# More tile buffers, another queue, a row sum on VectorE and another item order in the opening quarters of a decoder trunk

## The chip, the cores and the metric

The kernel runs on one core of a Trainium2 chip. The metric is device time in microseconds (us) of one execution; lower is better. A profiled execution gives the trace: one record for each instruction of TensorE (PE, with its weight loads as PEld), VectorE (DVE), ScalarE (ACT), GpSimd (POOL) and the DMA issues of SyncE (SP) and ACT. SPq and ACTq are the sequencers that issue DMAs.

## The reference, cut to what matters

A decoder trunk of two layers for one sequence of 256 tokens of width 2048, all in float32: layer 0 mixes with gated linear attention, layer 1 with latent attention, each followed by a gated feed-forward with a width-3 convolution. Every norm is modulated by a shift and a scale that come from a conditioning vector c:

```python
c_act = jax.nn.silu(c)
mod = c_act @ mod_w[i] + mod_b[i]          # (2048) @ (2048, 12288)
sh_m, sc_m, g_m, sh_f, sc_f, g_f = jnp.split(mod, 6, axis=-1)
h = modulate(rmsnorm(x, norm_mix_g[i]), sh_m, sc_m)   # h * (1 + scale) + shift
proj = h @ w_in                            # first product of layer 0
```

Here only the beginning counts: the shift and the scale of layer 0's first norm (two 2048 x 2048 blocks of mod_w, 32 MB), x normalised and modulated, and the first product with gla_w_in (q, then k). The convolution's taps and biases (ffn_conv_w, ffn_conv_b) are small and used much later.

## The kernel before, in words

**Precision.** A float32 product is three matmuls of rounded halves: w_hi (made by ACT, `hi`, line 746) and w_lo (made by DVE, `lo`, line 1166) of each weight item, h_hi and h_lo of the activations. A weight item is 4 row tiles by 512 columns, 1 MB, in a ring of four slots (`raw`); a load into a slot waits until the item four before it has been used (`load_item`, line 527).

**The opening.** It is divided into four quarters q, each for 512 of the 2048 columns of shift and scale. A quarter has eight modulation tiles of 1 MB, `PRE_TILES`: for each of four row groups i, kind 0 (shift) and kind 1 (scale). Tile m sits in slot m % 5; two slots are in `mods`, three in `pre_s2`. `load_pre` (line 545) waits, for tile m, until tile m - 5 has been consumed. Twenty of the 32 tiles are summed by DVE (`gather_pre`, lines 1347 and 1349): four instructions that multiply a row tile by a column of c and add it to `acc`. The other twelve, kind 1 with i < 3, are summed by TensorE (`pre_scale`, line 1944): eight records of one weight column against 512 columns, giving a row in PSUM.

At a quarter's end DVE copies TensorE's row to SBUF (`row_s`, line 1390), in space that x occupied. TensorE then adds up the 128 partitions of `acc` (`pre_reduce`, line 1956), for kind 0 and for kind 1; for kind 1 each of the four matmuls on `acc` is followed by a one-row matmul that adds `row_s` (line 1959). DVE turns both into the columns of `ab` (`pre_columns`, lines 1361 and 1363). ACT makes h_hi (line 761), DVE h_lo (lines 1240, 1245), for four row tiles of the input. With these, items 2q and 2q + 1 of gla_w_in can be multiplied (`q_item`).

**Order by hand.** Each engine has its own written-out order. DVE in quarter q: tiles 8q, 8q+2, 8q+4, `lo` of item 2q, tile 8q+6, `lo` of item 2q+1, tile 8q+7, the row, the columns, h_lo. TensorE: `pre_scale` 0, the first item of the quarter before, `pre_scale` 1, transposes of the normalised input, `pre_scale` 2, both reductions, the second item of the quarter before. SP issues all loads in one order: tiles 0, 1, then small rows and x, 2, 3, item 0, 4, 5, item 1, 6, 7, 8 to 11, item 2, 12, 13, item 3, 14, 15, then eight loads of the convolution's rows (each 88 rows of 512 bytes, 44 KB), 16 to 19, item 4, 20, 21, item 5, 22, 23, 24 to 27, item 6, 28, 29, item 7, 30, 31. ACT: squares of x, the normalised second half, then items 0 and 1 of `hi`, and so on.

After the quarters TensorE multiplies items 5, 6, 7, then the gate's item 8, and from item 9 on each item's load is released by the item four before it. The order after that is not touched.

Of the kernel before, what the change touches and what calls it, by code (L numbers as in the profile page):

```python
# [29 lines left out]
P = 128  # L30
RAW = 4
AHEAD = 3
MODS = 2
PRE = 5
KT_ITEM = 4
W = 512
ITEM = KT_ITEM * W
# [97 lines left out]
def yoco_kernel(nc, x, c, positions, mod_w, mod_b, norm_mix_g, norm_ffn_g, gla_w_in, gla_w_gate2,  # L135
# [49 lines left out]
    crow = place("crow", S2 + 2048, [KT, 2, P], F32)  # L185
    cvrow = place("cvrow", S2 + 4096, [2 * FT, 8, P], F32)
    pre_s2 = place("pre_s2", S2 + 8192, [P, PRE - MODS, D], F32)
    row_s = place("row_s", X, [1, W], F32)

    qk_t = place("qk_t", X, [P, 2 * DKT, T], F32)  # L190
    v_sb = place("v_sb", S2, [P, TT, D], F32)
# [115 lines left out]
    with ExitStack() as ctx:  # L307
# [6 lines left out]

        raw_in = [sem(f"raw_in{i}") for i in range(RAW)]
        mod_in = [sem(f"mod_in{i}") for i in range(MODS)]
        pre_in = [sem(f"pre_in{i}") for i in range(PRE)]
        pre_dve = sem("pre_dve")
        pre_pe = sem("pre_pe")
        pre_on = sem("pre_on")  # L320
# [91 lines left out]
                 "down10": 20, "down11": 24, "down12": 28, "end": 32}  # L412
        def pre_slot(m):

            k = m % PRE
            v = mods[:, k, :] if k < MODS else pre_s2[:, k - MODS, :]
            return v.rearrange("p (j n) -> p j n", j=KT_ITEM)

        PRE_TILES = [(q, i, kind) for q in range(4) for i in range(4) for kind in (0, 1)]

        def on_pe(m):
            _, i, kind = PRE_TILES[m]
# [87 lines left out]
        def _(sp):  # L510
# [18 lines left out]
            def load_mod(n, g, kt):  # L529

                if n < MODS:
                    sp.wait_ge(pre_dve, 20)
                else:
                    sp.wait_ge(mod_used, n - MODS + 1)
                w, col = mod_source(g)
                sp.dma_start(mods[:, n % MODS, :], w[kt * P:kt * P + P, col:col + D])\
                    .then_inc(mod_in[n % MODS], 16)

            def load_pre(m):

                if m >= PRE:
                    sp.wait_ge(pre_pe if on_pe(m - PRE) else pre_dve, taken(m - PRE))
                q, i, kind = PRE_TILES[m]
                w, col = mod_source(kind)
                sp.dma_start(pre_slot(m), columns(w, i, col + q * W)).then_inc(pre_in[m % PRE], 16)

            def columns(w, q, col, k_tiles=KT_ITEM, width=W):

# [53 lines left out]
            for n, src in enumerate(where):  # L602
                if n < 8:
                    for m in range(4 * n if n else 2, 4 * n + 4) if n % 2 == 0 else (4 * n, 4 * n + 1):
                        load_pre(m)
                if n - AHEAD == a["mla"].item + 2:

                    sp.wait_ge(tp_done, a["norm4"].tp + 2)
                for m in mod_at.get(n - AHEAD, ()):
                    load_mod(*m)  # L610
                if n == a["r"].item + 8:


                    sp.wait_ge(ms_done, made(a["diag"].ms + 1))
                    sp.wait_ge(xq_made, 2 * len(UNITS))
                    sp.dma_start(x_sb[:, :, :], x.rearrange("o (t p) d -> p (o t) d", p=P)).then_inc(x_in, 16)
                if n == a["down12"].item:

                    sp.wait_ge(mod_used, 12 * KT)
                    sp.dma_start(mods[:, 0, :], final_norm_g.partition_broadcast(P)).then_inc(fin_in, 16)  # L620
                load_item(n, src)
                if n < 8 and n % 2:
                    for m in (4 * n + 2, 4 * n + 3):
                        load_pre(m)
                if n == 3:
                    for layer in range(2):
                        for k in range(3):
                            sp.dma_start(cvrow[:, 4 * layer + k, :],
                                         ffn_conv_w[layer, k].rearrange("(r p) -> r p", p=P)).then_inc(taps_in, 16)
                        sp.dma_start(cvrow[:, 4 * layer + 3, :],  # L630
                                     ffn_conv_b[layer].rearrange("(r p) -> r p", p=P)).then_inc(taps_in, 16)
                if n == 8:

                    sp.dma_start(wg2[0:RANK, :], gla_w_gate2[0]).then_inc(wg_in, 16)
                    sp.dma_start(wg2[RANK:RANK + 1, :], gla_b_gate).then_inc(wg_in, 16)
# [98 lines left out]
        def _(act):  # L734
# [124 lines left out]
            act.wait_ge(x_in, 16)  # L859
            squares("norm0", x_sb, xn)  # L860
            normalised("norm0")
            for q in range(4):
                hi(2 * q)
                hi(2 * q + 1)
                if q < 3:
                    act.wait_ge(pre_on, q + 1)
                else:
                    act.wait_ge(columns_on, 1)
                split(a["norm0"].tp + 2 * q, 2, (h_hi,), (ab[:, A_OF["mix0"]],), (ab[:, A_OF["mix0"] + 1],), 2 * q)
                if q == 1:  # L870

                    act.wait_ge(ang_made, 1)
                    act.activation(sin[:, :, :], ang[:, 0], ACT.Sin).then_inc(sin_made, 1)
                    act.activation(cos[:, :, :], ang[:, 1], ACT.Sin).then_inc(sin_made, 1)
# [281 lines left out]
        def _(dve):  # L1156
# [180 lines left out]
            def gather_pre(m):  # L1337

                q, i, kind = PRE_TILES[m]
                dve.wait_ge(pre_in[m % PRE], 16 * (m // PRE + 1))  # L1340
                if taken(m) > 1:
                    dve.wait_ge(pre_dve, taken(m) - 1)
                total, tile_ = acc[:, kind, q * W:(q + 1) * W], pre_slot(m)
                for j in range(KT_ITEM):
                    ck = c_col[:, KT_ITEM * i + j:KT_ITEM * i + j + 1]
                    if j == 0 and (i == 0 or kind == 1):
                        ins = dve.tensor_scalar(total, tile_[:, j, :], ck, None, ALU.mult)
                    else:
                        ins = dve.scalar_tensor_tensor(total, tile_[:, j, :], ck, total, ALU.mult, ALU.add)
                    step.link(ins) if j < KT_ITEM - 1 else ins.then_inc(pre_dve, 1)  # L1350
# [23 lines left out]
            for q in range(4):  # L1374
                for i in range(4):
                    gather_pre(8 * q + 2 * i)
                    if q == 0 and i == 1:
                        dve.wait_ge(tp_done, 2)
                        for t, rows in enumerate((104, P, 96)):
                            ins = dve.tensor_copy(pcol[:, t, 0:rows], tp[:, 1, t * P:t * P + rows])  # L1380
                            step.mark(ins) if t < 2 else ins.then_inc(tp_free, 1)
                        dve.wait_ge(tp_free, 2)
                        normalised("norm0", x_sb, xn)
                    if i >= 2:
                        lo(2 * q + i - 2)
                gather_pre(8 * q + 7)
                if q == 0:
                    dve.wait_ge(xn_made, XN_FROM["norm0"] + TT)
                dve.wait_ge(pre_pe, 3 * q + 3)
                dve.tensor_copy(row_s[:, :], ms[0:1, (a["pre"].ms + 3 * q) % 2, :]).then_inc(ms_free, 1)  # L1390
                pre_columns(q)
                split("norm0", 2, (h_lo,), (h_hi,), (ab[:, A_OF["mix0"]],), (ab[:, A_OF["mix0"] + 1],), 2 * q)
                if q == 0:
                    angles()
                if q == 2:
                    dve.wait_ge(sin_made, 2)
                    step.link(dve.tensor_tensor(cos[:, :, :], cos[:, :, :], cos[:, :, :], ALU.mult))
                    step.link(dve.tensor_scalar(cos[:, :, :], cos[:, :, :], -2.0, 1.0, ALU.mult, ALU.add))
# [385 lines left out]
        def _(pe):  # L1784
# [150 lines left out]
            def pre_scale(q, i):  # L1935

                m = 8 * q + 2 * i + 1
                pe.wait_ge(pre_in[m % PRE], 16 * (m // PRE + 1))
                if i == 0:
                    pe.wait_ge(tp_free, 1)  # L1940
                o, tile_ = ms_open(a["pre"].ms + 3 * q), pre_slot(m)
                for j in range(KT_ITEM):
                    kt = KT_ITEM * i + j
                    ins = pe.matmul(o[0:1, :], c_col[:, kt:kt + 1], tile_[:, j, :], start=kt == 0,
                                    stop=kt == 3 * KT_ITEM - 1)
                ins.then_inc(pre_pe, 1)

            def pre_reduce(q):

                fill = a["pre"].ms + 3 * q + 1  # L1950
                for kind in range(2):
                    pe.wait_ge(pre_dve, 5 * q + 4 + kind)
                    o = ms_open(fill + kind)
                    for b in range(4):
                        c0 = q * W + b * P
                        ins = pe.matmul(o[:, b:b + 1], acc[:, kind, c0:c0 + P], ones[:, 0:1],
                                        start=True, stop=kind == 0)
                        if kind:
                            ins = pe.matmul(o[:, b:b + 1], row_s[0:1, b * P:(b + 1) * P], ones[0:1, 0:1],
                                            start=False, stop=True)  # L1960
                    ins.then_inc(ms_done, 1)

            def pre_turn(q):
# [14 lines left out]
            for q in range(4):  # L1978
# [3 lines left out]
                pre_scale(q, 1)  # L1982
                pre_turn(q)
                pre_scale(q, 2)
                pre_reduce(q)
                if q:
                    q_item(q - 1, 1)
            for ch in range(2):
                q_item(3, ch)

# [341 lines left out]
```

## Time and profile before

| | |
|---|---|
| median of 3 runs | 2476.84 us (2469.88 to 2478.08) |
| profiled execution | 2479.71 us |
| its span, first to last instruction | 2478.0 us |
| mean granted TensorE clock | 0.965 |
| TensorE busy | 95% |
| DVE busy | 74% |
| DMA | 255 GB/s on average |

The profiled execution's own time stands 1.7 us above its span and 2.9 us above the median of the runs. Its page gives busy time by engine, and the trace behind it answers for any stretch of time. The stretch of the change is 0 to 152 us: the four quarters end (second reduction read by DVE) at 47.9, 81.7, 113.1 and 143.6 us.

### The profile page before, as it was taken

How to read it: one execution, taken by the hardware profiler on the slowest of the kernel's cores; microseconds unless marked ns; L12 is line 12 of the kernel's file. 1: busy time of each engine (PE TensorE's matmuls, PEld its weight loads, DVE VectorE, ACT ScalarE, POOL GpSimd, SP SyncE). 2: the span in 40 equal slices, each digit the busy share in tenths (PEclk: the TensorE clock that was granted, in tenths of full speed). 3: DMA queues.
4: the chain of work that ended last, by engine and by line, in shares of the span. 5: the costliest groups of instructions: out<-in, count | busy, mean ns of one | idle time of the engine just before them, and what ended most of it. 6: DMA issues, size and time to landing. Idle time of an engine off the chain costs nothing.

```text
span 2478.0 us, 27045 instructions
## 1 busy us (share of the span) xinstructions
PE 2358.1 (95%) x10904; PEld 1912.0 (77%) x10904; DVE 1838.5 (74%) x1731; ACT 1102.2 (44%) x1195; POOL 114.7 (5%) x145
## 2 busy tenths in 40 slices
PE   5898999899999999999999899999999999999998
PEld 2567878577887788888887688877887888878876
DVE  5766987677888887878897878787777546555565
ACT  2124443334545335543444555435565345444453
POOL 0010650000000000000000000000000000000000
PEclk8898999898999999999999899998999999999999
DMA  8955769576997997869986656685866555555554
GB/s 322 336 202 220 257 236 371 189 277 235 359 334 272 340 354 279 327 243 367 343 315 244 220 174 213 247 321 186 325 252 239 184 194 182 186 172 190 187 174 148
DMA packets 259808, 632.91 MB, mean 255 GB/s; under 512 B 23505, under 2 KB 32745, under 8 KB 233978
## 3 DMA queue, kind: packets, MB, share of 16 engines
q1 hardware_dynamic: 258842, 626.26, 70.3%
q10 hardware_dynamic: 864, 5.24, 0.5%
q8 instruction: 70, 1.15, 0.2%
q14 instruction: 32, 0.26, 0.0%
HBM read 629.36 MB, written 2.10 MB: 255 GB/s over the span
## 4 chain that ended last, share of the span: by engine, by line
PE 78%; DVE 8%; DMA 7%; ACT 3%; issue 3%; SPq 1%; POOL 1%; DVEq 0%; POOLq 0%; ACTq 0%
PE gm L1805 21%; PE gm L1806 21%; PE gm L1812 20%; PE tp L1846 2%; PE gm L1797 2%; DMA raw<-in_ffn_w_down_dram 2%; PE gm L1799 2%; PE gm L1798 2%; DVE w_lo L1166 2%; ACT w_hi L746 2%; DVE acc L1183 2%; DVE conv L1546 1%; DMA raw<-in_gla_w_o_dram 1%; DMA mods<-in_mod_w_dram 1%; DMA raw<-in_gla_w_in_dram 1%
## 5 line engine op out<-in xcount | busy, mean ns | idle before, releaser
L1166 DVE TENSOR_TENSOR w_lo<-raw,w_hi 128x2048 fp32r<-128x2048 f32 (+1 forms) x378 | 851.3, 2255 | 375.5 <-ACT w_hi L746 374.3
L746 ACT ACTIVATE w_hi<-raw 128x2048 fp32r<-128x2048 f32 (+1 forms) x378 | 703.6, 1863 | 740.2 <-DMA raw<-in_ffn_w_up_dram 241.0
L1805 PE MATMUL gm<-w_hi,h_hi 128*128 128x512 f32 x1816 | 726.9, 400 | 0.2 <-DVE h_lo L1245 0.2
L1806 PE MATMUL gm<-w_hi,h_lo 128*128 128x512 f32 x1816 | 715.7, 394 | 0.0
L1812 PE MATMUL gm<-w_lo,h_hi 128*128 128x512 f32 x1816 | 448.8, 389 | 0.0
L1183 DVE SCALAR_TENSOR_TENSOR acc<-mods,c_col,acc 128x2048 f32<-128x2048 f32 x180 | 422.3, 2346 | 5.2 <-DMA mods<-in_mod_w_dram 4.6
L1805 PEld LDWEIGHTS gm<-w_hi,h_hi 128*128 128x128 f32 x1816 | 346.6, 191 | 77.1 <-issue 5.0
L1806 PEld LDWEIGHTS gm<-w_hi,h_lo 128*128 128x128 f32 x1816 | 346.3, 191 | 71.3 <-issue 1.0
L1812 PEld LDWEIGHTS gm<-w_lo,h_hi 128*128 128x128 f32 x1816 | 340.8, 188 | 70.9
L1805 PE MATMUL gm<-w_hi,a_hi 128*128 128x512 f32 x692 | 279.3, 404 | 11.7 <-DVE a_lo L1569 9.6
L1806 PE MATMUL gm<-w_hi,a_lo 128*128 128x512 f32 x692 | 274.9, 397 | 0.0
L1546 DVE SCALAR_TENSOR_TENSOR conv<-tp,cv_col,conv 128x255 f32<-128x255 f32 (+1 forms) x352 | 152.4, 477 | 85.2 <-ACT conv L982 82.0
L1812 PE MATMUL gm<-w_lo,a_hi 128*128 128x512 f32 x692 | 172.5, 390 | 0.0
L1805 PEld LDWEIGHTS gm<-w_hi,a_hi 128*128 128x128 f32 x692 | 133.0, 192 | 45.0 <-DVE a_lo L1569 12.6
L1806 PEld LDWEIGHTS gm<-w_hi,a_lo 128*128 128x128 f32 x692 | 133.1, 192 | 29.0 <-issue 1.4
L1812 PEld LDWEIGHTS gm<-w_lo,a_hi 128*128 128x128 f32 x692 | 130.3, 188 | 27.2
L752 ACT ACTIVATE u<-gm 128x1024 f32<-128x1024 f32 x76 | 77.4, 1019 | 152.8 <-PE gm L1812 145.5
L982 ACT ACTIVATE conv<-tp,cv_col 128x256 f32<-128x256 f32 x176 | 88.2, 559 | 119.6 <-PE tp L1846 119.2
L684 POOL TENSOR_TENSOR sq<-sq 128x2 f32<-128x2 f32 x4 | 4.6, 1156 | 1872.4 <-ACT tp L778 1872.4
L715 POOL TENSOR_TENSOR ex<-ex,qk_t 128x512 f32<-128x512 f32 x32 | 79.6, 2508 | 124.7 <-ACT ex L912 124.7
L761 ACT ACTIVATE h_hi<-tp,ab 128x256 fp32r<-128x256 f32 x64 | 32.0, 562 | 93.4 <-DVE ab L1363 55.7
L1797 PE MATMUL gm<-w_hi,h_hi 128*128 128x512 f32 x136 | 60.2, 442 | 10.2 <-DVE w_lo L1166 5.7
(257 smaller groups left out, 2166.4 us busy)
## 6 DMA issues: line engine op xcount, KB each, us to landing
raw<-in_ffn_w_up_dram SPq DMA_DIRECT2D x176, 1024.0 KB, 4.9
mods<-in_mod_w_dram SPq DMA_DIRECT2D x174, 1024.0 KB, 7.2
raw<-in_ffn_w_down_dram SPq DMA_DIRECT2D x64, 1024.0 KB, 5.2
raw<-in_gla_w_in_dram SPq DMA_DIRECT2D x48, 1024.0 KB, 5.3
mods<-in_kv_mod_w_dram SPq DMA_DIRECT2D x32, 1024.0 KB, 6.9
raw<-in_ffn_w_down_dram SPq DMA_DIRECT2D x32, 768.0 KB, 4.3
pre_s<-in_mod_w_dram SPq DMA_DIRECT2D x18, 1024.0 KB, 11.1
raw<-in_gla_w_o_dram SPq DMA_DIRECT2D x16, 1024.0 KB, 9.0
```

What stands on the lines that cost most here:

```text
L715: pool.tensor_tensor(f, f, s, ALU.mult).then_inc(xq_made, 1)
L746: act.activation(w_hi[:, k % RAW, 0:words], raw[:, k % RAW, 0:words], ACT.Copy).then_inc(hi_made, 1)
L752: act.activation(dst, gm[:, par] if src is None else src, func).then_inc(u_made, 1)
L982: ins = act.activation(conv[:, j % 2, side, :], tp[:, bank, side * T:(side + 1) * T], ACT.Identity, scale=cv_col[:, layer, 2, cs], bias=cv ...
L1166: dve.tensor_tensor(w_lo[:, k % RAW, 0:words], raw[:, k % RAW, 0:words], w_hi[:, k % RAW, 0:words].bitcast(F32), ALU.subtract).then_inc(lo ...
L1183: return dve.scalar_tensor_tensor(total, tile_, ck, total, ALU.mult, ALU.add)
L1546: ins = dve.scalar_tensor_tensor(v, tp[:, bank, side * T:(side + 1) * T - shift], cv_col[:, layer, tap, cs], v, ALU.mult, ALU.add)
L1797: pe.matmul(o, hi_s[:, kt, tok], wh[:, j, :], start=kt == 0, stop=False)
L1798: pe.matmul(o, hi_s[:, kt, tok], wl[:, j, :], start=False, stop=False)
L1805: pe.matmul(o, hi_s[:, kt, tok], wh[:, j, :], start=kt == 0, stop=False)
L1806: pe.matmul(o, lo_s[:, kt, tok], wh[:, j, :], start=False, stop=False)
L1812: return pe.matmul(o, hi_s[:, kt, tok], wl[:, j, :], start=False, stop=kt == total - 1)
```

## The change

The ring of modulation tiles gets two more slots, `pre_x`, in the space of x, which is free once x has been normalised. Tiles 0 to 9 keep their slots; tile 10 and 11 go to the new ones (after a wait until x has been read) and from tile 12 on a tile takes the slot of the tile seven before it. The eight loads of the convolution's rows leave SP's order and are issued by ACT, after the normalised input and before item 0's `hi`. `row_s` goes: DVE adds TensorE's row, which is in PSUM, into partition 0 of `acc`, and the reduction of kind 1 has no one-row matmuls; DVE first waits for its own last sum. In TensorE's order the second item of the quarter before comes ahead of the reductions in quarters 1 and 2, and stays behind them in quarter 3. The loads of the first two later modulation tiles wait for TensorE's last `pre_scale` too.

```diff
+PRE_LATE = 2
-    row_s = place("row_s", X, [1, W], F32)
+    pre_x = place("pre_x", X, [P, PRE_LATE, D], F32)
 def pre_slot(m):
-            k = m % PRE
-            v = mods[:, k, :] if k < MODS else pre_s2[:, k - MODS, :]
+            k = PRE_SLOT[m]
+            v = mods[:, k, :] if k < MODS else pre_s2[:, k - MODS, :] if k < PRE else pre_x[:, k - PRE, :]
+        PRE_SLOT = [m % PRE if m < 2 * PRE else (m - 2 * PRE + PRE) % (PRE + PRE_LATE) for m in range(len(PRE_TILES))]
+        def pre_landed(m):
+            return 16 * PRE_SLOT[:m + 1].count(PRE_SLOT[m])
 def load_mod(n, g, kt):
                 if n < MODS:
                     sp.wait_ge(pre_dve, 20)
+                    sp.wait_ge(pre_pe, 12)
 def load_pre(m):
-                if m >= PRE:
-                    sp.wait_ge(pre_pe if on_pe(m - PRE) else pre_dve, taken(m - PRE))
+                before = [k for k in range(m) if PRE_SLOT[k] == PRE_SLOT[m]]
+                if before:
+                    sp.wait_ge(pre_pe if on_pe(before[-1]) else pre_dve, taken(before[-1]))
+                elif PRE_SLOT[m] >= PRE:
+                    sp.wait_ge(xn_made, XN_FROM["norm0"] + TT)
 SP's order of loads
-                if n == 3:
-                    for layer in range(2):
-                        for k in range(3):
-                            sp.dma_start(cvrow[...], ffn_conv_w[layer, k]...).then_inc(taps_in, 16)
-                        sp.dma_start(cvrow[...], ffn_conv_b[layer]...).then_inc(taps_in, 16)
 ACT
             normalised("norm0")
+            for layer in range(2):
+                for k in range(3):
+                    act.dma_start(cvrow[...], ffn_conv_w[layer, k]...).then_inc(taps_in, 16)
+                act.dma_start(cvrow[...], ffn_conv_b[layer]...).then_inc(taps_in, 16)
 DVE, at a quarter's end
-                if q == 0:
-                    dve.wait_ge(xn_made, XN_FROM["norm0"] + TT)
+                dve.wait_ge(pre_dve, 5 * q + 5)
                 dve.wait_ge(pre_pe, 3 * q + 3)
-                dve.tensor_copy(row_s[:, :], ms[0:1, (a["pre"].ms + 3 * q) % 2, :]).then_inc(ms_free, 1)
+                row = acc[0:1, 1, q * W:(q + 1) * W]
+                dve.tensor_tensor(row, row, ms[0:1, (a["pre"].ms + 3 * q) % 2, :], ALU.add).then_inc(ms_free, 1)
 TensorE, pre_reduce
                         ins = pe.matmul(o[:, b:b + 1], acc[:, kind, c0:c0 + P], ones[:, 0:1],
-                                        start=True, stop=kind == 0)
-                        if kind:
-                            ins = pe.matmul(o[:, b:b + 1], row_s[0:1, b * P:(b + 1) * P], ones[0:1, 0:1],
-                                            start=False, stop=True)
+                                        start=True, stop=True)
 TensorE, order in a quarter
                 pre_scale(q, 2)
+                if 0 < q < 3:
+                    q_item(q - 1, 1)
                 pre_reduce(q)
-                if q:
-                    q_item(q - 1, 1)
+                if q == 3:
+                    q_item(2, 1)
```

The waits of `gather_pre` and `pre_scale` for a landed tile use `PRE_SLOT` and `pre_landed` in the same way.

## Rows read from the trace of the kernel before

**Rows 1.** The page: the span and TensorE's busy time.

```profile
span 2478.0 us, 27045 instructions
...
PE 2358.1 (95%) x10904; PEld 1912.0 (77%) x10904; DVE 1838.5 (74%) x1731; ACT 1102.2 (44%) x1195; POOL 114.7 (5%) x145
```

**Rows 2.** Busy time by stretch; the line with core 0 names the columns.

```profile
core 0: us, PE busy (x) PEld busy (x) DVE busy (x) ACT busy (x) POOL busy (x), PEclk, DMA share, GB/s
35.00:40.00 5.00, 1.86 (x8) 1.78 (x8) 4.89 (x5) 0.00 (x0) 0.00 (x0) 0.69 1.05 387
50.00:55.00 5.00, 4.75 (x15) 2.05 (x14) 4.58 (x14) 2.15 (x2) 0.00 (x0) 0.94 0.46 169
55.00:60.00 5.00, 5.00 (x21) 3.05 (x20) 4.68 (x9) 0.00 (x0) 0.00 (x0) 1.00 0.18 34
...
72.00:74.00 2.00, 1.65 (x8) 1.56 (x8) 2.00 (x2) 0.00 (x0) 0.00 (x0) 0.50 1.09 305
```

**Rows 3.** DVE's timeline, quarters: start, us, line, form, [idle before <-releaser].

```profile
34.85 3.11 DVE L1349 SCALAR_TENSOR_TENSOR acc<-mods,c_col,acc 128x512 f32<-128x512 f32 x4 [2.81 <-DMA mods<-in_mod_w_dram]
...
55.28 0.48 DVE L1347 TENSOR_SCALAR acc<-pre_s,c_col 128x512 f32<-128x512 f32 x1
...
86.72 0.49 DVE L1347 TENSOR_SCALAR acc<-mods,c_col 128x512 f32<-128x512 f32 x1
...
100.03 3.12 DVE L1349 SCALAR_TENSOR_TENSOR acc<-pre_s,c_col,acc 128x512 f32<-128x512 f32 x4 [1.83 <-DMA pre_s<-in_mod_w_dram]
...
108.03 0.67 DVE L1390 COPY row_s<-ms 1x512 f32<-1x512 f32 x1
...
113.09 0.16 DVE L1361 TENSOR_TENSOR modc<-ms,pcol 128x4 f32<-128x4 f32 x1 [4.33 <-PE ms L1959]
...
143.59 0.16 DVE L1361 TENSOR_TENSOR modc<-ms,pcol 128x4 f32<-128x4 f32 x1 [2.97 <-PE ms L1959]
```

**Rows 4.** The chain of waits, quarter 2's second reduction: start, us, what.

```profile
108.84 0.56 PE ms L1956 x2
...
112.48 0.51 PE ms L1959 x2
```

**Rows 5.** TensorE's timeline, quarters 1 and 2.

```profile
71.78 1.87 PE L1956 MATMUL ms<-ones,acc 128*128 128x1 f32 x8 [4.96 <-DVE acc L1349]
...
101.39 1.09 PE L1846 MATMUL tp<-ident,xn 128*128 128x128 f32 x8
102.41 3.59 PE L1944 MATMUL ms<-mods,c_col 128*1 128x512 f32 x8
105.94 1.05 PE L1956 MATMUL ms<-ones,acc 128*128 128x1 f32 x8
```

**Rows 6.** Busy time by stretch, items 2 (warm) and 5 (mostly half clock).

```profile
92.20:97.90 5.70, 5.70 (x26) 4.46 (x26) 5.49 (x6) 0.57 (x1) 0.00 (x0) 1.00 1.04 395
...
143.40:151.80 8.40, 8.40 (x25) 6.71 (x25) 4.12 (x9) 2.24 (x5) 2.44 (x12) 0.63 0.00 1
```

**Rows 7.** SP's issues: start, time from first to last in the merged row, line.

```profile
8.38 3.29 SPq L527 DMA_DIRECT2D raw<-in_gla_w_in_dram  x1
...
23.23 7.84 SPq L545 DMA_DIRECT2D pre_s<-in_mod_w_dram  x3
...
42.95 15.57 SPq L545 DMA_DIRECT2D pre_s<-in_mod_w_dram  x2
...
61.78 2.29 SPq L628 DMA_DIRECT2D cvrow<-in_ffn_conv_w_dram  x3
...
67.56 0.39 SPq L545 DMA_DIRECT2D mods<-in_mod_w_dram  x1
```

**Rows 8.** ACT's timeline, the first two items and one DMA issue.

```profile
24.00 1.91 ACT L746 ACTIVATE w_hi<-raw 128x2048 fp32r<-128x2048 f32 x1 [0.49 <-DMA raw<-in_gla_w_in_dram]
32.13 1.91 ACT L746 ACTIVATE w_hi<-raw 128x2048 fp32r<-128x2048 f32 x1 [6.22 <-DMA raw<-in_gla_w_in_dram]
...
357.88 0.39 ACTq L846 DMA_DIRECT2D gate_b<-in_mod_b_dram  x1
```

More of the change, by code:

```diff
@@ L316, in yoco_kernel @@
         mod_in = [sem(f"mod_in{i}") for i in range(MODS)]
-        pre_in = [sem(f"pre_in{i}") for i in range(PRE)]
+        pre_in = [sem(f"pre_in{i}") for i in range(PRE + PRE_LATE)]
         pre_dve = sem("pre_dve")
@@ L539, in load_pre @@
             def load_pre(m):
-                if m >= PRE:
-                    sp.wait_ge(pre_pe if on_pe(m - PRE) else pre_dve, taken(m - PRE))
+                before = [k for k in range(m) if PRE_SLOT[k] == PRE_SLOT[m]]
[3 more added lines that the diff above has]
+                    sp.wait_ge(xn_made, XN_FROM["norm0"] + TT)
                 q, i, kind = PRE_TILES[m]
                 w, col = mod_source(kind)
-                sp.dma_start(pre_slot(m), columns(w, i, col + q * W)).then_inc(pre_in[m % PRE], 16)
+                sp.dma_start(pre_slot(m), columns(w, i, col + q * W)).then_inc(pre_in[PRE_SLOT[m]], 16)
             def columns(w, q, col, k_tiles=KT_ITEM, width=W):
@@ L624, in _ @@
                         load_pre(m)
-                if n == 3:
-                    for layer in range(2):
-                        for k in range(3):
[L628 to L631, printed above, removed]
                 if n == 8:
@@ L861, in _ @@
             normalised("norm0")
+            for layer in range(2):
+                for k in range(3):
+                    act.dma_start(cvrow[:, 4 * layer + k, :],
+                                  ffn_conv_w[layer, k].rearrange("(r p) -> r p", p=P)).then_inc(taps_in, 16)
+                act.dma_start(cvrow[:, 4 * layer + 3, :],
+                              ffn_conv_b[layer].rearrange("(r p) -> r p", p=P)).then_inc(taps_in, 16)
             for q in range(4):
@@ L1339, in gather_pre @@
                 q, i, kind = PRE_TILES[m]
-                dve.wait_ge(pre_in[m % PRE], 16 * (m // PRE + 1))
+                dve.wait_ge(pre_in[PRE_SLOT[m]], pre_landed(m))
                 if taken(m) > 1:
@@ L1937, in pre_scale @@
                 m = 8 * q + 2 * i + 1
-                pe.wait_ge(pre_in[m % PRE], 16 * (m // PRE + 1))
+                pe.wait_ge(pre_in[PRE_SLOT[m]], pre_landed(m))
                 if i == 0:
```

## The prediction

> **What bounds the kernel now.** Read the page first: span 2478.0 us, TensorE busy for 95% of it [rows 1]. The change touches only the start (0 to about 152 us), so the next view is busy time by stretch there. The queues carry 387 GB/s when full; while quarter 0 ends and quarter 1 begins they carry 169 and then 34 [rows 2]. Two later gaps, near 85 and 120 us, look the same. One MB tile at 387 GB/s takes 2.71 us; ACT sees the same pace, since the first two weight items, three tiles apart, are converted at 24.00 and 32.13 [rows 8]. A quarter moves eight tiles and two items, 10 MB, so transfers alone would take 27.1 us. The quarters take 31.4 us: quarter 1's sums start at 55.28, quarter 2's at 86.72 [rows 3].
>
> DVE's timeline says why. Quarter 2's idle pieces are 1.83 us for a tile, 4.33 us for TensorE's second reduction and about 1.2 for ACT's h_hi; all else is DVE's own work [rows 3]. The queues go quiet because SP sits in front of tile 13, whose slot still holds tile 8: that pair of issues stretches over 15.57 us [rows 7]. Tile 8 is summed only at 55.28. So DVE sets the quarter, and late tiles cost it another 1.9 us. After the quarters everything is paced by items (item 9's load waits for item 5's matmuls), so I take what is gained by the end of item 5 as kept.
>
> I call T0 to T3 the ends of the second reductions. Before: T0 47.8, T1 81.6, T2 113.0 (112.48 + 0.51) [rows 4], T3 143.5 [rows 3]; item 5 ends at 151.8 [rows 6].
>
> **Convolution rows on ACT's queue.** Removed from SP: eight issues between 61.78 and 67.56, about 5.7 us [rows 7]. That is worth nothing alone: tile 16, queued behind them, is wanted only at 86.72. The transfers remain, and now start near 23.5 us instead of at an idle moment. Their price: two 2 us stretches, one of which stands in [rows 2], carry 305 GB/s at a full DMA share. The missing 82 GB/s over 4 us is 0.33 MB, to which come their own 0.35 MB (8 x 44 KB): 0.68 MB of queue time, 1.8 us. Quarter 0 is waiting for tiles just then (2.81 us idle until 34.85 [rows 3]), so I charge all 1.8 us to T0. Bounds: 0.9 (their bytes alone) and 3.7 (704 rows of 512 B, each as slow as one of the 512 rows of 2 KB in a tile's 2.71 us).
>
> The Trainium skill weighs in here: "DMA: Bandwidth & Descriptors", section "Issuing engines are not separate DMA queues", says that all issuers share the same DMA engines, so a second issuer saves only issue time. By it the rows cost the same 1.8 us; a free second path would make the sum 1.8 us better.
>
> Issuing costs ACT eight times 0.39 (its own DMA issue [rows 8]) to 0.76 (2.29 / 3, SP's [rows 7]), 3 to 6 us, in front of item 0's conversion at 24.00. Item 0 then ends by 32 and DVE subtracts it until 34; the next tile lands at 34.85 + 1.8. Hidden, with over 2 us spare. If that cover goes, see the second rival.
>
> **TensorE's row added by DVE.** Gone: eight thin 1-row matmuls, interleaved with eight real ones. The sixteen took 108.84 to 112.99, 4.15 us; the eight real ones alone take 1.87 at half clock and 1.05 at full [rows 4, 5]. The row copy (0.67) becomes an add with one operand in PSUM; a 128x512 subtraction beside it takes 0.69, so 0 to 0.1 more each, and the new wait on DVE's own sum some hundredths; together 0.3 us in all. Nothing but the reduction is queued behind that wait. So quarters 0 to 2 gain 2.1 (clock low) to 3.1 us (high). In quarter 3 the idle is only 2.97 [rows 3]; 1.1 to 2.2 remain, gain 0.8 to 1.8. T0: 47.8 + 1.8 - 2.1 = 47.5.
>
> **Two more buffers.** I walk the queue, one tile per 2.71 us. Tiles 10 and 11 need only x consumed (about 23.5); tile 12 waits for tile 5, 13 for 6, and from there each for the one seven before it. In the new schedule tile 14's slot is free at about 45, when the queue still holds work until 61; tile 15 waits for tile 8, summed at 58, queue filled until 64; tile 22 waits at 75, filled until 88; tile 31 waits for tile 24 at 112, filled until 118. No gap opens, and the tiles that DVE waited for land before their use: tile 14 at 64 for 66.5, tile 22 at 91 for 93.4, tile 30 at 118 for 120. The three late-tile stops (about 1.9 each [rows 3]) go. What is late next is TensorE, by little. Bounds: 0 (tiles as late as before) to 5.7 us gained.
>
> The waits for landed tiles keep their number. SP's extra wait in front of the first later modulation tile is for TensorE work over since the quarter's end: 0.
>
> **Item order.** Items 1 and 3 move ahead of the reductions, into TensorE's idle time (4.96 us before the first reduction of quarter 1 [rows 5]), on the fast clock that follows the scale matmuls. Item 1 frees its slot some 16 us earlier. The price is that quarter 2's TensorE chain becomes full: h_lo ready at T1 + 5.2, item 2 5.66 [rows 6], scale 3.53, transposes 1.02, scale 3.53 [rows 5], item 3 5.66, two reductions 2.1: T1 + 26.7. DVE's side is 31.4 - 1.9 - 3.1 = 26.4. TensorE ends last by 0.3 us.
>
> **The sum.** T1: T0 + 33.8 (81.6 - 47.8) - 1.9 - 2.1 to 3.1 = 76.3 to 77.3. T2: + 26.7 = 103.0 to 104.0. T3: + 30.5 (143.5 - 113.0) - 1.9 - 0.8 to 1.8 = 129.8 to 131.8, and 0.3 for the adds. That is 11.4 to 13.4 us earlier. Item 5, still after the reduction, took 8.4 us at a clock of 0.63, item 2 5.7 at 1.00 [rows 6]. In quarter 3 TensorE again has an idle stretch of about 5 us before the second reduction, so I leave it cold with a gain of 0 to 1.2 (item 1 took 7.2 at 0.78, after a similar gap). Total 11.4 to 14.6; I take 12.5. The profiled execution took 2479.7, so 2467.2; the median of the runs shown is 2.9 us lower, so 2464.3. I write 2465.
>
> **Rivals.** *Tiles stay late.* The leads above are only about 2 us. If the queues lose more than that (SP's in-order waits, slow small rows), the 5.7 us come back, and 6 to 7 us of gain remain: 2470.5. For it: every tile in question is issued a few us before it is wanted. Against: the queue never runs dry in my walk.
>
> *ACT is held at its issues.* While the queues are backed up, SP's issues take 2.6 us each (7.84 / 3), one 3.29 [rows 7]. If ACT's eight are held as long, item 0 is converted at 23.5 + 8t, and with the conversion, subtraction, tile 6, item 1, tile 7, row and reduction behind it (15.1 us) T0 is 38.6 + 8t. It decides from t = 1.1; at 2.7 the whole gain is gone (2477); at 3.3 T0 is 65.0, 17.5 late, and the kernel 5 us slower: 2482. More than 0.3% slower needs 3.6. For it: ACT issues just inside the backlog. Against: ACT's queue is empty then, and its one issue shown takes 0.39 with traffic about.
>
> [...]
>
> *The clock stays high.* If TensorE is fast through quarter 3, item 5 takes 5.7: 2.7 us instead of 0 to 1.2. Time 2462.
>
> **How the numbers follow.** About 0.3%, 7.4 us, is what a measurement of this kernel can tell from no change. Forecast 0.64, tiles late 0.15, ACT held 0.10, clock high 0.06, and 0.05 for a start that changes nothing for reasons I don't see. Faster by over 7.4 us: nearly all of the first and fourth, and a third of the second, 0.74. Slower by over 7.4: 0.04, out of the ACT case and the rest. Same: 0.22. The unchanged kernel's own runs spread over 8 us, so the range is 2457 to 2475, reaching over the tiles-late case and leaving the held ACT outside.
>
> **What would show it.** The second reductions in 1.1 to 2.1 us with no thin matmuls; DVE's idle before modc near 1.3 to 2.3; no tile waits after 36 us; DMA share full from 5 to about 121 us; T0 near 47.5, T3 near 131, item 5's end near 139. First waits of DVE for tile 6 about 1.8 us later than before. I am wrong if item 0's conversion starts after 33, if tile waits remain in quarters 1 to 3, or if item 9 lands no earlier relative to the start by 12 us.

## The result and the profile after

The changed kernel took 2455.3 us (median of six executions) against 2471.7 of six of the kernel before; the ratio is 0.9934, interval 0.991 to 0.9957, so 10.6 to 22.2 us faster. Run a second time it took 2459.0 against 2470.7, ratio 0.9951 (0.9932 to 0.9969), by the ratio 12.1 us faster. The forecast was 2465 with a range from 2457: the direction was right, and the first measured time lies 1.7 us below the range.

| | before | after |
|---|---|---|
| profiled execution | 2479.7 | 2452.9 |
| end of reductions read by DVE, quarters 0 to 3 | 47.9, 81.7, 113.1, 143.6 | 47.8, 77.4, 104.2, 132.0 |
| SP issues item 9 (item 5 used) | 152.0 | 139.6 |
| DVE copies the gate's rows (first thing behind the opening) | 168.6 | 156.1 |
| from there to the end of the span | 2309.4 | 2294.8 |

The two copies of the gate's rows, before and after:

```profile
168.56 0.41 DVE L1411 COPY g_t<-ms 16x256 f32<-16x256 f32 x1 [1.77 <-PE ms L2025]
...
156.13 0.41 DVE L1420 COPY g_t<-ms 16x256 f32<-16x256 f32 x1 [1.82 <-PE ms L2033]
```

The opening gave 12.4 us. The two spans (2478.0 and 2450.9) differ by 27.1; the other 14.7 us lie in code that the change does not touch. I call the time from that copy to the end of the span the rest.

Busy time by stretch of the changed kernel (columns: stretch, its length, TensorE busy and its count, granted clock, DMA share, GB/s) answers [rows 2]:

```profile
50.00:55.00 5.00, 5.00 (x15) 0.91 1.05 388
55.00:60.00 5.00, 5.00 (x20) 1.00 1.05 384
85.00:115.00 30.00, 28.37 (x114) 1.00 1.05 387
120.00:125.00 5.00, 3.81 (x15) 1.00 0.21 40
```

Where the queues had carried 169 and 34 GB/s they carry 388 and 384, and the 30 us around quarter 2 are full throughout. The queues run down early in the 120 to 125 stretch; the walk along the queue had their end at 121.

DVE's timeline answers [rows 3]:

```profile
36.92 3.12 DVE L1358 SCALAR_TENSOR_TENSOR acc<-mods,c_col,acc 128x512 f32<-128x512 f32 x4 [4.58 <-DMA mods<-in_mod_w_dram]
...
47.80 0.16 DVE L1370 TENSOR_TENSOR modc<-ms,pcol 128x4 f32<-128x4 f32 x1 [2.02 <-PE ms L1965]
...
77.42 0.16 DVE L1370 TENSOR_TENSOR modc<-ms,pcol 128x4 f32<-128x4 f32 x1 [2.02 <-PE ms L1965]
...
101.96 0.68 DVE L1399 TENSOR_TENSOR acc<-acc,ms 1x512 f32<-1x512 f32 x1
103.26 0.16 DVE L1370 TENSOR_TENSOR ab<-ms,pcol 128x4 f32<-128x4 f32 x1 [0.62 <-PE ms L1965]
104.22 0.16 DVE L1370 TENSOR_TENSOR modc<-ms,pcol 128x4 f32<-128x4 f32 x1 [0.80 <-PE ms L1965]
...
132.00 0.16 DVE L1370 TENSOR_TENSOR modc<-ms,pcol 128x4 f32<-128x4 f32 x1 [2.02 <-PE ms L1965]
```

The wait for tile 6 has grown from 2.81 to 4.58 us; it is the only wait for a tile from there to the quarters' end. The second reduction costs DVE 2.02 us in quarters 0, 1 and 3, where it had cost 4.33, 4.33 and 2.97. In quarter 2 DVE waits 0.62 us for the first reduction (ahead of `ab`) and 0.80 for the second: TensorE comes later there, as forecast.

TensorE's timeline (L1965 is the reduction) answers [rows 4, 5]:

```profile
72.18 0.95 PE L1965 MATMUL ms<-ones,acc 128*128 128x1 f32 x8
75.48 1.84 PE L1965 MATMUL ms<-ones,acc 128*128 128x1 f32 x8 [2.36 <-DVE ab L1370]
...
102.28 1.84 PE L1965 MATMUL ms<-ones,acc 128*128 128x1 f32 x16
...
130.06 1.83 PE L1965 MATMUL ms<-ones,acc 128*128 128x1 f32 x8 [4.71 <-DVE ab L1370]
```

A reduction of eight records lasts 0.95 us at 2.4 GHz and 1.84 at 1.2 GHz; the two of quarter 2 follow item 3 without a pause and take 1.84 together. In quarters 1 and 3 the engine was idle for 2.36 and 4.71 us before the second one, and the clock was low again.

ACT's timeline answers [rows 8], with its first DMA issue:

```profile
21.46 1.37 ACTq L867 DMA_DIRECT2D cvrow<-in_ffn_conv_w_dram  x3
...
24.90 1.91 ACT L749 ACTIVATE w_hi<-raw 128x2048 fp32r<-128x2048 f32 x1 [1.44 <-DMA raw<-in_gla_w_in_dram]
34.21 1.91 ACT L749 ACTIVATE w_hi<-raw 128x2048 fp32r<-128x2048 f32 x1 [7.41 <-DMA raw<-in_gla_w_in_dram]
```

The eight issues, 21.46 to 24.85, take 0.31 to 0.62 us each, though SP's own take 2.8 and, on average, 3.2 us each then. They even start while ACT's activation of 21.45 runs. Item 0 is converted 0.9 us later than before.

### The profile page after: what moved, and what is told of

The parts are those of the page before. It is cut to its first block, busy times and chain, and to the rows that moved or that the text cites. A ratio compares the mean times of both kernels' runs of the same rounds, so it can differ in the third digit from the quotient of the medians.

```text
span 2450.9 us, 26986 instructions
## 1 busy us (share of the span) xinstructions
PE 2334.3 (95%) x10872; PEld 1892.1 (77%) x10872; DVE 1838.1 (75%) x1731; ACT 1102.2 (45%) x1195; POOL 117.8 (5%) x145
## 4 chain that ended last, share of the span: by engine, by line
PE 75%; DVE 11%; DMA 6%; issue 3%; ACT 3%; SPq 1%; POOL 0%; DVEq 0%; POOLq 0%; ACTq 0%
PE gm L1814 20%; PE gm L1815 20%; PE gm L1821 20%; DVE w_lo L1175 2%; PE tp L1855 2%; DVE acc L1192 2%; DMA raw<-in_ffn_w_down_dram 2%; PE gm L1806 2%; PE gm L1807 2%; PE gm L1808 2%; ACT w_hi L749 2%; DVE acc L1358 1%; DMA raw<-in_gla_w_o_dram 1%; DVE conv L1555 1%; DMA mods<-in_mod_w_dram 1%
## 5 line engine op out<-in xcount | busy, mean ns | idle before, releaser
L1814 PE MATMUL gm<-w_hi,a_hi 128*128 128x512 f32 x692 | 277.8, 401 | 12.1 <-DVE a_lo L1578 9.1
L1555 DVE SCALAR_TENSOR_TENSOR conv<-tp,cv_col,conv 128x255 f32<-128x255 f32 (+1 forms) x352 | 152.3, 477 | 88.6 <-ACT conv L991 85.4
L755 ACT ACTIVATE u<-gm 128x1024 f32<-128x1024 f32 x76 | 77.5, 1019 | 152.0 <-PE gm L1821 145.9
```

Source lines behind the costliest of these rows:

```text
L755: act.activation(dst, gm[:, par] if src is None else src, func).then_inc(u_made, 1)
L1555: ins = dve.scalar_tensor_tensor(v, tp[:, bank, side * T:(side + 1) * T - shift], cv_col[:, layer, tap, cs], v, ALU.mult, ALU.add)
L1814: pe.matmul(o, hi_s[:, kt, tok], wh[:, j, :], start=kt == 0, stop=False)
```

## The experiments

Each comparison is of interleaved executions of both kernels on the same chip, in five rounds; the third profiles are single executions. A gain in the opening is read from one profile of each kernel. "Opening" is the time of the gate's copy in the profile: 168.6, 168.5 and 168.1 in three profiles of before, 156.1, 155.1 and 156.6 in three of the changed kernel, means 168.4 and 155.9. The diffs show the lines that matter, with ... for what lies between.

### Both kernels again

No edit.

> The kernel before, unchanged, run again, to see how much of a difference comes without any change. Profiles of before and after so far: item 5 ends at 151.8 and 139.4 us, the rest (from there to the end of the span) is 2326.2 and 2311.5 us. Theory A (the opening gives 12.4, the rest differs because TensorE's clock spells fall differently from one execution to the next): item 5 ends within 0.5 us of 151.8, but the rest may lie anywhere from about 2308 to 2327; ratio 1.000 within 0.002. Theory B (the change itself also shortens the rest): item 5 at 151.8 and the rest again at 2323 or more.

Measured: ratio to before 1.0012 (0.9999 to 1.0025), opening 168.5, rest 2299.0.

> The changed kernel, unchanged, run again. Both theories: item 5 ends at 139.4 within 0.5. Theory A: the ratio comes nearer to 12.4 us of about 2472, 0.9950, and the rest may lie from 2308 to 2327. Theory B: ratio 0.9934 or lower again, 16 us or more, and a rest below 2314.

Measured: ratio 0.9951 (0.9932 to 0.9969), opening 155.1, rest 2301.5. SP issues item 9 at 138.6, 1.0 us earlier than in the first profile, where I had allowed 0.5: quarter 1's second reduction takes 1.02 us here instead of 1.84. Ratio and rest fit theory A in both runs. The same kernel before has rests 10.4 us apart, and the changed kernel's second rest is longer than before's second. A single profile's rest says nothing about the change.

### The row added by DVE, alone

```diff
 before.py
-                if q == 0:
-                    dve.wait_ge(xn_made, XN_FROM["norm0"] + TT)
-                dve.tensor_copy(row_s[:, :], ms[0:1, ...]).then_inc(ms_free, 1)
+                dve.wait_ge(pre_dve, 5 * q + 5)
+                row = acc[0:1, 1, q * W:(q + 1) * W]
+                dve.tensor_tensor(row, row, ms[0:1, ...], ALU.add).then_inc(ms_free, 1)
 ...
-                        if kind:   # one-row matmuls
-                            ins = pe.matmul(o[:, b:b + 1], row_s[...], ones[0:1, 0:1], ...)
```

> Before with one part of the change: DVE adds TensorE's row, no one-row matmuls. Theory by parts: tiles are late as before, so the reductions give 2.1 us in quarters 0 to 2 and 0.9 in quarter 3, but a quarter that starts sooner waits longer for its tiles (SP is held by DVE's sums, which move with it, so most is kept): item 5 ends 5 to 7.5 us earlier, 144.3 to 146.8. Rival (transfers set the quarters): the waits for tiles grow by what the reductions save, and item 5 ends at most 3 us earlier, 149 or later.

Measured: ratio 0.9970 (0.9954 to 0.9986), item 9 issued at 144.1, opening 160.6: 7.8 us earlier. DVE's timeline:

```profile
45.93 0.16 DVE L1360 TENSOR_TENSOR modc<-ms,pcol 128x4 f32<-128x4 f32 x1 [2.02 <-PE ms L1955]
...
66.68 3.12 DVE L1348 SCALAR_TENSOR_TENSOR acc<-pre_s,c_col,acc 128x512 f32<-128x512 f32 x4 [1.91 <-DMA pre_s<-in_mod_w_dram]
...
96.01 3.11 DVE L1348 SCALAR_TENSOR_TENSOR acc<-pre_s,c_col,acc 128x512 f32<-128x512 f32 x4 [1.94 <-DMA pre_s<-in_mod_w_dram]
...
125.98 3.11 DVE L1348 SCALAR_TENSOR_TENSOR acc<-mods,c_col,acc 128x512 f32<-128x512 f32 x4 [2.82 <-DMA mods<-in_mod_w_dram]
```

The 7.8 us are 0.3 above my best case. Quarter 0 ends 2.0 us earlier, and the waits for tiles hardly grow in quarters 1 and 2 (1.91 and 1.94 us against 1.86 and 1.83) and by 1.0 us in quarter 3 (2.82 against 1.80; the kernel before had up to 2.60 for such a wait in its second profile): SP is released by DVE's sums, so it moves with them. The rival, transfers that set the pace, is out.

### The two buffers, alone

```diff
 after.py, with the row copy, the one-row matmuls, SP's
 convolution rows and the old item order of before put back
+    row_s = tmp("row_s", 5120, [1, W], F32)   # x's space holds tiles now
```

> Before with one part of the change: the two more tile buffers and their waits (the row copy is kept, in another place; convolution rows stay in SP's order; old item order). Theory by parts: the three waits of 1.9 us for tiles go, item 5 ends 5 to 6.5 us earlier, 145.3 to 147, and the queues never run dry before 121. Rival (buffers are idle as long as DVE sets the pace): less than 2 us.

Measured: ratio 0.9974 (0.9961 to 0.9987), item 9 issued at 144.4, opening 160.9: 7.5 us earlier, 1.0 more than my best case. DVE waits for no tile after 36 us; the reductions still take their time:

```profile
79.69 0.16 DVE L1372 TENSOR_TENSOR modc<-ms,pcol 128x4 f32<-128x4 f32 x1 [4.33 <-PE ms L1968]
...
108.03 0.16 DVE L1372 TENSOR_TENSOR modc<-ms,pcol 128x4 f32<-128x4 f32 x1 [2.63 <-PE ms L1968]
...
137.18 0.16 DVE L1372 TENSOR_TENSOR modc<-ms,pcol 128x4 f32<-128x4 f32 x1 [2.31 <-PE ms L1968]
```

Quarter 1 ends 2.0 us earlier and quarter 3 is 1.35 us shorter, about the waits for tiles; quarter 2 is 3.1 us shorter, since its reductions cost DVE 2.9 instead of 4.3 us (the clock is high for part of them), and item 5 takes 7.2 us instead of 8.4 for the same reason. The 1.4 us of quarter 2 were in no term of mine; a gain of 0 to 1.2 in item 5 was in the sum, but not charged to the buffers.

### Where and when the convolution rows are loaded

```diff
 after.py
             normalised("norm0")
-            (eight act.dma_start of cvrow)
 ...
             hi(8)
+            (eight act.dma_start of cvrow)
```

> The changed kernel with the convolution rows' eight loads issued by ACT after quarter 3, when the queues are empty. Theory (the rows cost 1.8 us in quarter 0, where tiles are waited for): the end of quarter 0's reduction goes from 47.7 to 45.9, and item 5's end from 139.4 to 137.6. Rival (quarter 0 isn't bound by the queue's bytes, or the later quarters take it back because tiles are then late): item 5's end stays within 0.5 us of 139.4.

```diff
 after.py
-            (eight act.dma_start of cvrow)
 SP, after tiles 14 and 15
+            (eight sp.dma_start of cvrow)
```

> The changed kernel with the convolution rows back in SP's order behind tile 15. Theory: T0 1.8 us earlier (45.9); the rows then take 1.8 us of queue time and SP's issues about 5 us between tiles 15 and 16, when the queue is some 8 us ahead of SP, so no wait of more than 1 us follows; item 5's end 137.6 to 138.6. Rival (the leads of about 2 us are used up): a tile wait of 1 to 3 us in quarter 1 or 2 and item 5's end at 139.4 or later.

Measured: late on ACT, ratio 0.9920 (0.9903 to 0.9938), item 9 issued at 137.8, opening 154.3; in SP's order, ratio 0.9931 (0.9911 to 0.9950), item 9 issued at 138.0, opening 154.5. DVE's timeline with the rows late:

```profile
34.58 3.11 DVE L1358 SCALAR_TENSOR_TENSOR acc<-mods,c_col,acc 128x512 f32<-128x512 f32 x4 [2.82 <-DMA mods<-in_mod_w_dram]
...
45.45 0.16 DVE L1370 TENSOR_TENSOR modc<-ms,pcol 128x4 f32<-128x4 f32 x1 [2.02 <-PE ms L1965]
```

Tile 6 is there 2.3 us earlier (34.58 against 36.92, wait 2.82) and quarter 0 ends 2.35 us earlier (45.45, in SP's order 45.73). So loading the rows amid quarter 0 costs 2.1 to 2.35 us at T0; behind the opening 1.4 to 1.6 are left against the mean. In SP's order they cause one wait of 0.42 us. The executions don't tell these kernels from the changed one: the intervals overlap. So the place that the change gives the rows, amid quarter 0, is the part of it that costs time in the opening. It is the moment and not ACT's queue: late on ACT they cost no more than in SP's order.

### The old item order

```diff
 after.py
-                if 0 < q < 3:
-                    q_item(q - 1, 1)
                 pre_reduce(q)
-                if q == 3:
-                    q_item(2, 1)
+                if q:
+                    q_item(q - 1, 1)
```

> The changed kernel with the old item order: items 1 and 3 after both reductions. Theory: items 1 and 3 then run behind the reduction, at the low clock for part, and end some 13 us later in each quarter than h_lo needs: quarter 2's TensorE chain gets item 1 (5.7 to 7.2) in front of its scale matmuls, 3.5 + 7 = 10.8 before item 2 in place of 5.2, so its end moves by up to 5 us; quarter 3's the same through item 3. Item 5's end 4 to 10 us later, 143.5 to 149. Rival (the order is worth nothing, TensorE has idle time enough): within 1 us of 139.4.

Measured: ratio 0.9940 (0.9922 to 0.9958), item 9 issued at 138.2, opening 154.7, 0.4 to 1.9 us earlier than the changed kernel's three. The rival holds, all but 0.2 us: the order gains nothing, and in this one profile it costs a little. My expectation counted item 1 as added to quarter 2's chain and forgot that item 3 leaves it at the other end. The first lines of TensorE's timeline show the one item behind T1, the next two quarter 2's reductions at once after the scale matmuls, the last two quarter 3's reductions:

```profile
75.66 1.84 PE L1965 MATMUL ms<-ones,acc 128*128 128x1 f32 x8 [4.32 <-DVE ab L1370]
...
84.55 3.59 PE L1953 MATMUL ms<-pre_x,c_col 128*1 128x512 f32 x8
...
98.29 3.59 PE L1953 MATMUL ms<-pre_s,c_col 128*1 128x512 f32 x8
101.81 2.17 PE L1965 MATMUL ms<-ones,acc 128*128 128x1 f32 x16
...
128.39 1.05 PE L1965 MATMUL ms<-ones,acc 128*128 128x1 f32 x8
129.94 1.02 PE L1965 MATMUL ms<-ones,acc 128*128 128x1 f32 x8 [0.50 <-DVE ab L1370]
```

The chain is equally long: DVE reads T2 at 104.1 against 104.2. The difference comes in quarter 3. With item 3 in it TensorE is busy up to the reductions; the second one starts after 0.50 us idle and takes 1.02 us. In the changed kernel item 3 has left that quarter, TensorE idles 4.71 us and the same reduction takes 1.83.

### Item 5 too ahead of the reductions

```diff
 after.py, with the rows late
                 pre_scale(q, 2)
-                if 0 < q < 3:
+                if q:
                     q_item(q - 1, 1)
                 pre_reduce(q)
-                if q == 3:
-                    q_item(2, 1)
```

> The changed kernel with the convolution rows late (as in the one above) and item 5 too ahead of quarter 3's reductions. Theory: TensorE's idle 5 us in quarter 3 take up item 5; the second reduction then ends at about the same time (130), and item 6 starts with h_lo, 5.2 us later, so item 6 starts at 135.2 in place of 137.6 (e3) or 139.4 (changed kernel): the start of item 6 another 2 to 3 us earlier than in e3, in all 4 to 5 us faster than the changed kernel in the opening. Rival: item 5 delays the reductions (TensorE busy until after the row add), and nothing is gained over e3.

> The kernel with the rows late and all items ahead of the reductions, run again beside the next one. In its first profile the gate's copy (the first instruction of DVE behind the opening) stood at 151.3 us, against 168.5 of before and 155.1 to 156.1 of the changed kernel, but its ratio (0.9921) was that of the kernel without item 5's move (0.9920, copy at 154.3). Theory A (what differs is TensorE's time at the low clock behind the opening, about 0.48 us of rest for each us; it was 111 us there and 95 in the other): the copy again at 151.3, low-clock time anywhere from 89 to 124 us, ratio nearer to 17.2 us, 0.9930 or lower. Theory B (item 5's move makes the rest slower): rest again at 2306 or more.

Measured: ratios 0.9921 (0.9906 to 0.9936) and 0.9934 (0.9917 to 0.9952), openings 151.3 and 152.3, rests 2306.9 and 2303.1. TensorE's timeline:

```profile
125.04 0.94 PE L1965 MATMUL ms<-ones,acc 128*128 128x1 f32 x8
126.47 1.02 PE L1965 MATMUL ms<-ones,acc 128*128 128x1 f32 x8 [0.48 <-DVE ab L1370]
```

The idle 4.71 us before the second reduction are 0.48, its 1.83 us are 1.02. The opening is 2.1 to 3.1 us shorter than with the rows late alone, as expected, but neither ratio shows it (0.9920 with the rows late alone). The second run decides between its two theories only in part: the opening is 1.0 us later than theory A had it, the ratio at the edge of A's, and the rest below B's 2306. The worth of item 5's move by executions stays unproved.

### `lo` in the gap of the reduction

```diff
 the kernel above
-                    if i >= 2:
-                        lo(2 * q + i - 2)
+                    if i == 2:
+                        lo(2 * q)
 ...
                 dve.tensor_tensor(row, row, ms[0:1, ...], ALU.add).then_inc(ms_free, 1)
+                lo(2 * q + 1)
                 pre_columns(q)
```

> As the one above, and DVE makes w_lo of the quarter's second item (2.2 us) behind the row add, in the gap in which it waits for the second reduction. Theory: the gap of 1.2 to 2.0 us is filled, quarter 0 ends 2 us earlier; from quarter 2 on TensorE's chain of 26.4 to 26.7 us a quarter is the bound, so in all the gate's copy comes 2 to 3.5 us earlier, 147.8 to 149.3. Rival 1 (transfers bound, leads used up): tile waits of 1 to 3 us return in quarters 1 to 3 and less than 1 us is gained. Rival 2 (DVE still bound in every quarter): 6 us or more, 145 or earlier.

Measured: ratio 0.9911 (0.9894 to 0.9928), 2451.3 us, opening 149.7, 1.6 to 2.6 us earlier but 0.4 later than my latest. DVE reads the second reductions at 44.0, 71.9, 98.9 and 126.0. Its timeline shows the first rival beside the theory:

```profile
89.81 3.12 DVE L1358 SCALAR_TENSOR_TENSOR acc<-pre_s,c_col,acc 128x512 f32<-128x512 f32 x4 [1.41 <-DMA pre_s<-in_mod_w_dram]
...
116.91 3.11 DVE L1358 SCALAR_TENSOR_TENSOR acc<-pre_s,c_col,acc 128x512 f32<-128x512 f32 x4 [0.99 <-DMA pre_s<-in_mod_w_dram]
```

The last two quarters take 27.0 and 27.1 us, which is what 10 MB of transfers take (27.1), and waits for tiles are back. This version has the lowest median; its ratio lies below the changed kernel's two, though its interval overlaps the first, and those with the rows late (0.9920, 0.9921) too.

### Third profiles

> The kernel before, a third profile, for the low-clock time and the rest. Profiles so far, counted from the gate's copy to the end: before 2309.4 us with 124 us at the low clock, and 2299.0 with 102; the changed kernel 2294.8 with 93, and 2301.5 with 104. Theory A: rest = 2250 + 0.48 times the low-clock time within 3 us, whichever kernel it is. Theory B (the change shortens the rest): 2304 or more with no such relation.

> The changed kernel, a third profile. Theory A: the same relation, rest = 2250 + 0.48 times the low-clock time within 3 us; opening's copy at 155 to 156.2. Theory B: rest 2298 or less again.

Measured: openings 168.1 and 156.6, rests 2305.2 and 2301.8, low-clock times 111 and 99 us. Theory A's formula misses by 2.1 and 4.3 us, the second outside my 3; theory B, which wanted a rest of 2298 or less for the changed kernel, misses by more than 3 there too. The opening of 156.6 is 0.4 above what I had expected. Over all fourteen profiles (kernels with the same code behind the opening) a straight line fitted afterwards gives rest = 2257.4 + 0.42 times the low-clock time, correlation 0.88, scatter 2.1 us. Low-clock time is a stretch's length times 2 x (1 - granted clock), summed over the forty equal stretches of the rest.

| profile | low-clock us | rest us |
|---|---|---|
| before, three | 124, 102, 111 | 2309.4, 2299.0, 2305.2 |
| after, three | 93, 104, 99 | 2294.8, 2301.5, 2301.8 |
| row only; buffers only | 115; 89 | 2301.5; 2291.7 |
| rows late; old order; rows on SP | 95; 105; 95 | 2298.6; 2302.1; 2298.4 |
| all items first, two; `lo` in the gap | 111, 114; 107 | 2306.9, 2303.1; 2301.1 |

One such place (columns as above), in the kernel before and, 12.4 us earlier, in the changed one:

```profile
180.00:190.00 10.00, 8.21 (x27) 0.85 0.77 280
190.00:200.00 10.00, 10.00 (x37) 0.80 0.28 98
```

```profile
167.60:177.60 10.00, 8.21 (x32) 1.00 0.75 276
177.60:187.60 10.00, 10.00 (x46) 1.00 0.47 162
```

The granted clock is 0.85 and 0.80 in one and 1.00 in the other, and TensorE gets through 64 matmul records in one and 78 in the other.

## Why the prediction was right and where it was wrong

**The schedule was right.** T0 to T3 were forecast at 47.5, 76.3 to 77.3, 103.0 to 104.0 and 130.1 to 132.1; the trace has 47.7, 77.3, 104.1 and 131.9 (each 0.1 before DVE's read), T2 0.1 past its range. Item 5's end was forecast 11.4 to 14.6 us earlier and came 12.4 earlier. The causes were told apart by part-kernels: the row 7.8 us (forecast 7 to 10), the buffers 7.5 (forecast 5.7, and the clock gains told above), the convolution rows against it, 1.4 to 1.6 at the end (1.8). These sum to 13.8. The kernel with the old item order consists of just these three parts, and its opening came 13.7 earlier: the parts add up. With the new order it is 12.4.

**The item order was misjudged.** The sum charged it 0.3 us in quarter 2 and gave it no gain; I kept it as a use of TensorE's idle time and, ahead of its run, thought it worth 4 to 10 us. It gained nothing. The old order's opening was even 0.4 to 1.9 us earlier, since item 3 had kept TensorE busy, and quarter 3's second reduction short (1.02 instead of 1.83 us).

**ACT was not held.** Its issues took 0.31 to 0.62 us, below the 1.1 from which that rival decides. The rows' price at T0 was 2.1 to 2.35 us where I had 1.8. The Trainium skill's page "DMA: Bandwidth & Descriptors", section "Issuing engines are not separate DMA queues", says that DMAs of all issuers run on the same DMA engines. The trace agrees: issued by ACT, the rows delayed SP's tile 6 by 2.3 us.

**The step that failed is the last one of the sum**: "The profiled execution took 2479.7, so 2467.2; the median of the runs shown is 2.9 us lower, so 2464.3. I write 2465." The base was mis-sized. The three executions shown had a median of 2476.8; six give 2471.7, twenty-nine 2470.7. Of the 9.7 us between 2465 and 2455.3 the base makes 5.1, the rounding 0.7, and 3.9 are what the first comparison shows beyond the 12.5 us of the sum; the last are open. From 2471 the same 12.5 us lead to 2458.5, within 0.5 us of the second measurement and 3.2 above the first. The profiled execution was slower than nearly all others of its kernel; TensorE spent 124 us behind the opening at the low clock, the most of fourteen profiles. The range, 2457 to 2475, took in the spread of the executions upwards, where the rivals were, and left only 8 us below.

**What stays open.** Whether the first comparison's 16.4 us, 4 more than the opening gave, are chance. Its interval reaches down to 10.6, and the second has 12.1, so chance is enough. But the mean rest of three profiles is 5 us longer for before than for after (2304.6, 2299.4); with a spread of 2291.7 to 2309.4 over all kernels three cannot decide it. In the eight comparisons of the changed kernel and its variants the gain by the ratio exceeds the gain of the opening by 2.2 us on average (-0.3 to 5.7); in the two part-kernels it falls short by 0.4 and 1.1. An effect of some 2 us behind the opening is thus neither shown nor excluded. What sets where the clock falls was not tried.

## What to carry to other kernels

Take the base of a forecast from many executions, not from the profiled one or from three, and give the range the spread of that base on both sides; one profile's difference in untouched code is no effect. When a sequencer waits in order for slots that a slower engine frees, count the buffers by walking the queue tile by tile: here it had the issue of tile 31 at 112 and the queues' end at 121, and the trace has 112.6 and shortly after 120. A small transfer cost the critical path when it was queued in the one stretch where tiles were being waited for, and hardly anything where the queue was ahead of its users or dry. Before an item is moved out of a quarter, ask whether it was what kept its engine busy up to the reduction.

## What the runs showed of the hardware

- A matmul with one row took as long as one with 128: 0.51 us a pair against 0.51 to 0.56 at 1.2 GHz [rows 4]. Removing eight such records a quarter cut DVE's wait from 4.33 to 2.02 us in quarters 0 and 1.
- DMA issues on ACT ran beside its own activation (issue at 21.46, activation 21.45 to 23.45) and took 0.31 to 0.62 us each beside SP's backlog, where one issue took 2.8 to 3.2 us.
- 0.36 MB in rows of 512 bytes, loaded amid the tiles, delayed tile 6 by 2.3 us; 1 MB in rows of 2 KB takes 2.71.
- After 4.7 us idle the granted clock was low for the next reduction (1.83 us); after 0.5 us idle it was not (1.02). After 2.4 us idle it was low (1.84 us). The time at the low clock behind the opening ranged from 89 to 124 us in fourteen profiles of kernels with the same code there.
